# Fused transformer and RWKV-7 step on one core: the first preparation's products two gate tiles later, the wait for the gate stores moved past a barrier

## The chip, the cores and the metric

One core of one Trainium2 chip runs the whole step as one program. The metric is the device time of one execution in microseconds (us), lower is better, as the median of several runs.

## The reference

One trunk layer of a hybrid network over 512 latent and 128 context tokens with width 1024. What matters here is its first half:

```
h = modulate(rmsnorm(x))
proj = h @ w_in                      # q, k, v | u (RWKV inputs) | ga, gr (gates)
attn_o = block_attention(q, k, v)
rwkv_o = rwkv7_bidirectional(u)      # decays, rates, normed keys, then a scan per direction
merged = sigmoid(ga) * (attn_o @ w_attn_br) + sigmoid(gr) * (rwkv_o @ w_rwkv_br)
x = x + gate1 * (merged @ w_out)     # then a gated MLP in the same manner
```

## The kernel before

Activations lie feature-major: 128 features on the partitions, 644 token columns. A dense product is made in tiles of 128 output features. Each fp32 operand is split into a high and a low part, and one tile is 8 input blocks x 3 part products x 2 column halves = 48 matmuls (line 669). Two tiles make a block, whose 1 MB of weights SyncE loads into one of two buffers, ScalarE (ACT) copies to the high part (`next_hi`, L1155) and VectorE (DVE) turns into the low part (`next_lo`, L1471).

The program is written by hand, engine by engine; each engine runs its own list in order and waits on semaphores. `phase_over` (L449 to L452) is a barrier of TensorE (PE), ACT, DVE and GpSimd (POOL): each drains, adds one, and waits for all four. Barrier 1 stands ahead of the dense products of `w_in`. These are 6 tiles of q, k, v, 14 tiles of u, and, last, 16 tiles of gates in 8 blocks, numbered t = 0 to 15 here. Barrier 2 follows them, then comes the first half of the RWKV recurrence (`chunks(0)`), then barrier 3 and the attention.

Between the gate tiles the kernel prepares the recurrence of the first half (*the first preparation*, `it` = 0). PE makes ten small products of 640 columns (`prepare_product`, L933 and L934). Products 0 and 1 are sums of squared keys, one for each of two head groups, and read what ACT squares in `key_squares` once the keys have been reloaded from DRAM (`uc<-u_scratch`). Products 2 to 9 are four pairs, each pair a decay and a rate for one head group and one direction. The work of ACT and DVE on them is placed by the same tile number t:

- ACT, after it has evacuated tile 0: `key_squares`. After tile 1: `key_norm_log` (L1249) and `key_norm` (L1254) for both groups, from products 0 and 1. After tiles 2, 4, 6, 8: the tanh of both products of a pair (`prep_tanh`, L1263) and `key_factor` (L1270). After tiles 3, 5, 7, 9: `prep_decays`, three exponentials (L1277 to L1279).
- DVE at even t: `next_lo` of the next block, and at t = 2 to 9 parts of `prepare(0)` (L1595 to L1633).

PSUM holds two tiles. PE may begin tile t only when ACT has evacuated tile t-2 (L678: `pe.wait_ge(tile_evac, 2 * b + j + 1)`; ACT counts up in L1292). The list of ACT, which the change leaves as it is, is (L1283 to L1307, `g_st` being the stores of the gates):

```python
        for b in range(NBLK_U + NBLK_Q, BLK_BR):
            if b + 1 < BLK_BR:
                next_hi(b + 1, (b + 1) % 2)
            for j in range(2):
...
                ac.wait_ge(tile_done, 2 * b + j + 1)
                if f >= 1:
                    ac.wait_ge(g_st[j], 16 * f)
                ac.activation(gout[j][:, :], tile(2 * j), ACT.Tanh, scale=0.5).then_inc(tile_evac, 1)
...
                elif t < 10 and t % 2 == 0:
                    for n in range(2):
                        prep_tanh(0, t // 2 - 1, n)
                    key_factor(0, t // 2 - 1)
```

`prep_tanh` and `key_norm_log` begin with a wait for their product (`pe_prep`). Behind each evacuation POOL issues the store of the gate tile to DRAM (L614), 16 in all; their buffers `gout` are not written again before barrier 3.

Of the kernel before, what the change touches and what calls it, by code (L numbers as in the profile page):

```python
# [42 lines left out]
NBLK_U, NBLK_Q, NBLK_G = 7, 3, 8  # L43
# [110 lines left out]
def build(nc, io):  # L154
# [25 lines left out]
    def sem(name):  # L180
        return ctx.enter_context(nc.semaphore(name))
# [228 lines left out]
    g_st = [sem(f"gates_stored{s}") for s in range(2)]  # L410
# [38 lines left out]
    def phase_over(eng, n):  # L449

        eng.drain().then_inc(barrier, 1)
        eng.wait_ge(barrier, 4 * n)  # L452
# [20 lines left out]
    def paired(names):  # L473

        return [(g, name, s) for g, name in in_order(names) for s in range(2)]
# [5 lines left out]
    def at_stage(names, it, g, name):  # L481
        count = COUNT[id(names)]
        return it * len(count) + count[g, name]
# [97 lines left out]
    @block.gpsimd  # L581
    def _(gp):
        phase_over(gp, 1)
        for kv in range(2):
            gp.dma_start(k2[:, kv, 512:768], ck_d[kv]).then_inc(cache_ld, 16)
        gp.dma_start(vo[:, 4:6, :, 64:128], cv_d.rearrange("p t (g n) -> p t g n", g=2)).then_inc(cache_ld, 16)
        for a in (0, 128):
            gp.memset(vo[:, :, :, a:a + 64].rearrange("p t g n -> p (t g) n"), 1.0).then_inc(ones_set, 1)
        for i in range(6):
            for s in range(2):  # L590
                gp.wait_ge(conv_done, 2 * i + s + 1)
                gp.dma_start(u_s[2 * i + s], uout[s][:, :]).then_inc(u_st[s], 16)
        gp.wait_ge(qst_done, 5)
        gp.dma_start(qa_s[:, 0:QK], qa_made[:, 0:QK]).then_inc(qa_st[0], 16)
        gp.dma_start(nk_d, qkv[:, 4, C0:C0 + CTX]).then_inc(kv_st, 16)
        gp.dma_start(nv_d, qkv[:, 5, C0:C0 + CTX]).then_inc(kv_st, 16)
        gp.dma_start(qc_s, qkv[:, 0:4, C0:C0 + CTX]).then_inc(qa_st[1], 16)
        gp.wait_ge(vt_copied, 1)
        gp.wait_ge(cache_ld, 48)
        gp.wait_ge(ones_set, 2)  # L600
        gp.dma_start(qa_s[:, QK:QA], qa_made[:, QK:QA]).then_inc(qa_st[1], 16)
        gp.wait_ge(kv_st, 32)
        gp.wait_ge(qa_st[0], 16)
        for s in range(2):
            gp.wait_ge(u_st[s], 16 * 6)
        gp.wait_ge(qa_st[1], 32)
        u_of = u_s.rearrange("(j h) p n -> h p j n", j=3)
        for s in range(2):
            gp.dma_start(hpw[s][:, :], hpw_d[s]).then_inc(rw_ld[0][s], 16)
            gp.dma_start(uc[s][:, :, :], u_of[s]).then_inc(rw_ld[0][s], 16)  # L610
        for i in range(NBLK_G):
            for s in range(2):
                gp.wait_ge(tile_evac, 2 * i + s + 2 * (NBLK_U + NBLK_Q) + 3)
                gp.dma_start(gate_s[i, :, s, :], gout[s][:, :]).then_inc(g_st[s], 16)  # L614
        for s in range(2):
            gp.wait_ge(g_st[s], 16 * NBLK_G)
        phase_over(gp, 2)

        def presets(it):
            for g, name, s in paired(PO_ST):  # L620
                if g >= 2:
                    gp.wait_ge(pe_g[s], at_stage(PE_ST, it, g - 2, "U1"))
                gp.tensor_copy(rm[s][g % 2][:, :, :, :].rearrange("p d q n -> p (d q) n"),
                               i64.unsqueeze(1).broadcast_to([P, 4, CH])).then_inc(po_g[s], 1)

        presets(0)
        phase_over(gp, 3)
        gp.wait_ge(o_copied, 10)
        gp.dma_start(br_s[0:4].rearrange("k p n -> p k n"), aT[:, :, :]).then_inc(a_st, 16)
        gp.wait_ge(a_st, 16)  # L630
        phase_over(gp, 4)
        presets(1)
        phase_over(gp, 5)
        for k in range(8):
            if k in (4, 5):
                gp.wait_ge(rw_st[k - 4], 32)
            gp.dma_start(bld[k][:, :], br_s[k]).then_inc(b_ld[k], 16)
        for f in range(KD):
            if f >= 2:
                gp.wait_ge(mf_done, f - 1)  # L640
            gp.dma_start(gld[f % 2][:, :, :], gate_s[f]).then_inc(gl_ld[f % 2], 16)
        gp.wait_ge(tile_done, 2 * BLK_OUT)
        gp.wait_ge(mf_done, KD)
        gp.wait_ge(m_lo, KD)
        gp.dma_start(x1[:, :, :], x_d).then_inc(x1_ld, 16)
        phase_over(gp, 6)
# [3 lines left out]
    def _(pe):  # L650
# [267 lines left out]
        def prepare_product(it, n):  # L918

            tb = tbs[it]  # L920
            pe.wait_ge(prep_read, 10 * it + n + 1 + it)
            if n < 2:
                pe.wait_ge(ac_prep, 8 * it + n + 1)
                w, x = blk1, tb[8 * n][:, :]
            else:
                s = (n - 2) // 4
                pe.wait_ge(rw_ld[it][s], 32)
                pe.wait_ge(low_done, 1)
                d, low = (n - 2) % 4 // 2, n % 2
                rows = slice(64 * low, 64 * low + 64)  # L930
                w, x = wcur[s][rows, d, :], wdad[rows, :]
            at = 3072 if it else 2048 + 1024 * (n % 2)
            pe.matmul(psf[:, at:at + 512], w, x[:, 0:512], start=True, stop=True)  # L933
            pe.matmul(psf[:, at + 512:at + T], w, x[:, 512:T], start=True, stop=True).then_inc(pe_prep, 1)  # L934

        def between_gates(t):

            if t == 1:
                for s in range(2):
                    prepare_product(0, s)  # L940
            elif t % 2 == 0 and 2 <= t < 10:
                for j in range(2):
                    prepare_product(0, t + j)

        for b in range(NBLK_Q + NBLK_U, BLK_BR):
            dense_block(b, b % 2, hhi, hlo, lambda j: between_gates(2 * (b - NBLK_Q - NBLK_U) + j))
# [1040 lines left out]
```

## Time and profile before

| What | Value |
|---|---|
| median of 3 runs | 1492.28 us (1489.19 to 1492.94) |
| profiled execution: its own time, its span | 1493.71 us, 1491.9 us |
| TensorE granted clock, mean | 0.946 of full |
| busy: PE, DVE, ACT, POOL | 1336.6, 748.4, 530.3, 41.8 us |
| gate tiles, from the end of u's tiles to barrier 2 | about 208.9 to 346.2 us of the span |

The profile is one execution. Times in it count from the first instruction. The profiled execution's own time lies 1.8 us above its span (work around the instructions), and 1.4 us above the median of the runs. "PE L669 x48" is one tile.

### The profile page before, as it was taken

To read this page: it belongs to the slowest core of one execution; us is meant where nothing else is said; L and a number is where in the kernel's file an instruction comes from. 1 tells how busy PE (TensorE), PEld (TensorE's weight loads), DVE (VectorE), ACT (ScalarE), POOL (GpSimd) and SP (SyncE) were. 2 spreads that over 40 slices of the span, in tenths; PEclk is the share of its full clock that TensorE was granted. 3 is DMA by queue.
4 is the path that set the end of the run, shared out by engine and by line. 5 is a ranking of instruction groups with operands and counts; after the bars stand their busy time and mean duration, and the time that the engine had idled before them with its cause. 6 is when DMAs were issued, how large, how long until landed. Compare 5 with 4: busy or idle time off the path is not lost.

```text
span 1491.9 us, 31857 instructions
## 1 busy us (share of the span) xinstructions
PE 1336.6 (90%) x13967; PEld 1231.7 (83%) x13967; DVE 748.4 (50%) x1114; ACT 530.3 (36%) x794; POOL 41.8 (3%) x84
## 2 busy tenths in 40 slices
PE   5799998997998799879985989799999999799993
PEld 2799997997997455479965968599999999799992
DVE  3517644623554489954554622465545455344445
ACT  3535535411334343223243211363333334233332
POOL 0000010000000000000001000000000000000000
PEclk8799999998999799989996999999999999899996
DMA  9222373313000200020006477012122121022221
GB/s 397 66 94 92 105 277 128 104 54 157 8 4 3 85 0 1 1 94 8 4 11 246 145 284 294 25 61 85 60 81 84 56 84 42 14 70 78 70 64 71
DMA packets 24761, 134.58 MB, mean 90 GB/s; under 512 B 2992, under 2 KB 3632, under 8 KB 16208
## 3 DMA queue, kind: packets, MB, share of 16 engines
q1 hardware_dynamic: 19088, 103.59, 19.5%
q0 software_dynamic: 5568, 29.40, 5.2%
q8 instruction: 89, 1.46, 0.4%
q14 instruction: 16, 0.13, 0.0%
HBM read 112.66 MB, written 20.32 MB: 89 GB/s over the span
## 4 chain that ended last, share of the span: by engine, by line
PE 80%; DVE 8%; DMA 5%; ACT 3%; issue 2%; PEld 1%; POOL 0%; POOLq 0%; PEldq 0%; DVEq 0%; SPq 0%; ACTq 0%
PE ps L669 43%; PE ps L1106 10%; PE ps L822 3%; PE ps L810 3%; PE ps L790 2%; PE ps L1009 2%; PE ps L704 1%; PE ps L968 1%; PE ps L802 1%; DMA xT<-in_x 1%; DVE rden L1761 1%; PE ps L986 1%; PE ps L694 1%; PE ps L933 1%; DMA bld<-branch_scratch 1%
## 5 line engine op out<-in xcount | busy, mean ns | idle before, releaser
L669 PE MATMUL ps<-h2lo,whi 128*128 128x322 f32 x672 | 154.5, 311 | 0.7 <-ACT facc L1193 0.7
L669 PE MATMUL ps<-h2hi,wlo 128*128 128x322 f32 x672 | 155.0, 312 | 0.0
L669 PE MATMUL ps<-h2hi,whi 128*128 128x322 f32 x672 | 154.0, 310 | 0.0
L1471 DVE TENSOR_TENSOR wlo<-raw,whi 128x2048 fp32r<-128x2048 f32 x48 | 109.7, 2287 | 72.0 <-ACT whi L1155 71.8
L669 PE MATMUL ps<-hlo,whi 128*128 128x322 f32 x544 | 128.2, 317 | 1.0 <-ACT qkv L1219 1.0
L669 PE MATMUL ps<-hhi,wlo 128*128 128x322 f32 x544 | 125.8, 312 | 0.0
L669 PE MATMUL ps<-hhi,whi 128*128 128x322 f32 x544 | 125.0, 311 | 0.0
L669 PEld LDWEIGHTS ps<-h2hi,whi 128*128 128x128 f32 x672 | 114.2, 190 | 0.0
L669 PEld LDWEIGHTS ps<-h2lo,whi 128*128 128x128 f32 x672 | 113.0, 189 | 0.9 <-DVE wlo L1471 0.9
L669 PEld LDWEIGHTS ps<-h2hi,wlo 128*128 128x128 f32 x672 | 113.6, 189 | 0.0
L1515 DVE SCALAR_TENSOR_TENSOR facc<-fraw,par,facc 128x642 f32<-128x642 f32 x44 | 39.0, 887 | 140.1 <-ACT facc L1193 140.1
L1155 ACT ACTIVATE whi<-raw 128x2048 fp32r<-128x2048 f32 x48 | 91.8, 1914 | 26.4 <-PE ps L669 15.8
L1192 ACT ACTIVATE fraw<-ps 128x644 f32<-128x644 f32 x44 | 31.2, 710 | 183.8 <-PE ps L669 182.5
L669 PEld LDWEIGHTS ps<-hlo,whi 128*128 128x128 f32 x544 | 91.9, 190 | 4.1 <-issue 2.4
L669 PEld LDWEIGHTS ps<-hhi,whi 128*128 128x128 f32 x544 | 92.7, 190 | 0.0
L669 PEld LDWEIGHTS ps<-hhi,wlo 128*128 128x128 f32 x544 | 92.2, 190 | 0.0
L1106 PE MATMUL ps<-dlo,whi 128*128 128x322 f32 x352 | 81.6, 314 | 10.1 <-DVE dlo L1885 8.9
L1106 PE MATMUL ps<-dhi,wlo 128*128 128x322 f32 x352 | 82.2, 315 | 0.0
L1106 PE MATMUL ps<-dhi,whi 128*128 128x322 f32 x352 | 81.3, 312 | 0.0
L1884 DVE TENSOR_TENSOR wlo<-raw,whi 128x512 fp32r<-128x512 f32 x44 | 30.4, 692 | 92.3 <-ACT dhi L1431 92.3
L1661 DVE COPY_PREDICATED tm<-con,ps 128x256 f32<-128x256 int32 x80 | 35.5, 444 | 68.7 <-PE ps L822 67.8
L1106 PEld LDWEIGHTS ps<-dlo,whi 128*128 128x128 f32 x352 | 59.8, 192 | 10.8 <-issue 10.8
(298 smaller groups left out, 2675.2 us busy)
## 6 DMA issues: line engine op xcount, KB each, us to landing
raw<-in_wblk SPq DMA_DIRECT2D x48, 1024.0 KB, 4.8
adl<-in_wada SPq DMA_DIRECT2D x8, 2048.0 KB, 8.7
raw<-in_wdn SPq DMA_DIRECT2D x44, 256.0 KB, 2.6
adaw<-in_wada SPq DMA_DIRECT2D x4, 2048.0 KB, 17.7
gate_scratch<-gout POOLq DMA_DIRECT2D x16, 322.0 KB, 2.8
gld<-gate_scratch POOLq DMA_DIRECT2D x8, 644.0 KB, 4.2
attention_inputs_used<-attention_scratch SPq DMA_DIRECT2D x1, 5056.0 KB, 14.6
u_scratch<-uout POOLq DMA_DIRECT2D x12, 320.0 KB, 2.4
```

The lines of the kernel that those rows point to most:

```text
L669: mm = pe.matmul(o, w, v, start=first, stop=last and w is hi and x is xh[n])
L790: mm = pe.matmul(bank(b, P, P * (2 * d + q))[r], src[r, d, tokens(d, q)], ar[s][r, d, chunk_of(g, d, q), :, :].rearrange("p a n -> p (a n) ...
L810: mm = pe.matmul(bank(b1, CH, CH * (2 * d + q))[r], abm[s][g % 2][r, d, q, 0, :], tm[s][r, d, q, :], start=True, stop=True)
L822: mm = pe.matmul(bank(b0, CH, CH * (2 * d + q))[r], left, right, start=True, stop=True)
L1009: mm = pe.matmul(bank(4 + h % 2), vo_u[:, c, h // 4, at:at + P], pt[h % 2][:, c, :], start=c == 0, stop=c == 5)
L1106: mm = pe.matmul(o, w, v, start=(k == 0 and q == 0), stop=(k == FF - 1 and q == 2))
L1155: ac.activation(whi[s][:, :], raw[s][:, :], ACT.Copy).then_inc(hi_done, 1)
L1192: ac.activation(fr[j][:, :], tile(2 * j), ACT.Copy)
L1471: TT(wlo[s][:, :], raw[s][:, :], whi[s][:, :].bitcast(F32), ALU.subtract).then_inc(lo_done, 1)
L1515: st.last(STT(fa[j][:, 1:TP - 1], fr[j][:, 0:TP - 2], taps(0), fa[j][:, 1:TP - 1], ALU.mult, ALU.add))
L1661: ins = dv.copy_predicated(t1[:, :, :, :], lev[:, l - 1].unsqueeze(2).broadcast_to(each), steps_of(bank(b0, 4 * CH)))
L1884: TT(wlo[s][:, 0:512], raw[s][:, 0:512], whi[s][:, 0:512].bitcast(F32), ALU.subtract)
```

## The change

On PE, each use of `prepare_product` between the gate tiles moves two tiles down: products 0 and 1 from behind tile 1 to behind tile 3, the pairs from behind tiles 2, 4, 6, 8 to behind tiles 4, 6, 8, 10. The lists of ACT and DVE stay. On POOL, the wait for the stores of the gates moves from ahead of barrier 2 to behind the presets of `chunks(0)` (copies of an identity matrix, L623), ahead of barrier 3.

```diff
@@ gpsimd
                 gp.dma_start(gate_s[i, :, s, :], gout[s][:, :]).then_inc(g_st[s], 16)
-        for s in range(2):
-            gp.wait_ge(g_st[s], 16 * NBLK_G)
         phase_over(gp, 2)
...
         presets(0)
+        for s in range(2):
+            gp.wait_ge(g_st[s], 16 * NBLK_G)
         phase_over(gp, 3)
@@ tensor
         def between_gates(t):
 
-            if t == 1:
+            if t == 3:
                 for s in range(2):
                     prepare_product(0, s)
-            elif t % 2 == 0 and 2 <= t < 10:
+            elif t % 2 == 0 and 4 <= t < 12:
                 for j in range(2):
-                    prepare_product(0, t + j)
+                    prepare_product(0, t - 2 + j)
```

## Rows read from the trace of the kernel before

**Rows 1.** The page's part 4, the chain that ended last, by engine:

```profile
PE 80%; DVE 8%; DMA 5%; ACT 3%; issue 2%; PEld 1%; POOL 0%; POOLq 0%; PEldq 0%; DVEq 0%; SPq 0%; ACTq 0%
```

**Rows 2.** The chain in order of time, gate tiles: start, us, what:

```profile
229.05 0.84 ACT tb L1241
...
232.49 7.93 PE ps L669 x48
240.43 1.07 PE ps L933 x4
...
256.20 1.06 PE ps L933 x4
...
289.03 50.23 PE ps L669 x336
...
339.29 0.72 ACT gout L1292
...
340.29 2.46 DMA gate_scratch<-gout
...
342.84 3.34 POOLq L451
```

**Rows 3.** Timeline of TensorE: start, us, engine, line, what, [idle before <-releaser]:

```profile
226.33 1.12 PE L933 MATMUL ps<-tb,con 128*128 128x512 f32 x2 [3.16 <-ACT tb L1241]
...
230.02 2.04 PE L933 MATMUL ps<-tb,con 128*128 128x512 f32 x2 [2.14 <-ACT tb L1241]
...
232.83 0.74 PE L669 MATMUL ps<-hhi,wlo 128*128 128x322 f32 x2
233.37 0.74 PE L669 MATMUL ps<-hhi,whi 128*128 128x322 f32 x2
```

**Rows 4.** Timeline of ACT, gate tiles:

```profile
229.79 0.69 ACT L1292 ACTIVATE gout<-ps 128x644 f32<-128x644 f32 x1
230.49 1.28 ACT L1249 ACT_TABLE_LOAD   x1
231.78 1.45 ACT L1249 ACTIVATE tb<-ps 128x640 f32<-128x640 f32 x2
...
241.74 0.80 ACT L1263 ACTIVATE tb<-ps,hw 128x640 f32<-128x640 f32 x1 [0.57 <-PE ps L934]
...
243.31 0.93 ACT L1270 ACTIVATE tb<-tb,kfc 128x640 f32<-128x640 f32 x1
...
250.33 0.74 ACT L1278 ACTIVATE tb<-tb 128x650 f32<-128x650 f32 x1
```

**Rows 5.** Timeline of DVE, gate tiles:

```profile
237.75 2.29 DVE L1471 TENSOR_TENSOR wlo<-raw,whi 128x2048 fp32r<-128x2048 f32 x1 [19.21 <-ACT whi L1155]
...
245.07 0.82 DVE L1610 TENSOR_TENSOR tb<-tb 128x640 f32<-128x640 f32 x1
...
246.54 0.82 DVE L1619 SCALAR_TENSOR_TENSOR tb<-tb,tb 128x640 f32<-128x640 f32 x1
251.18 0.83 DVE L1628 SCALAR_TENSOR_TENSOR ar<-tb,tb 128x640 f32<-128x640 f32 x1 [3.82 <-ACT tb L1278]
...
254.13 2.28 DVE L1471 TENSOR_TENSOR wlo<-raw,whi 128x2048 fp32r<-128x2048 f32 x1
```

**Rows 6.** Timeline of TensorE, two products of 640 columns at full clock:

```profile
472.52 1.13 PE L908 MATMUL ps<-ysum,con 128*128 128x512 f32 x2
...
473.71 1.02 PE L908 MATMUL ps<-ysum,con 128*128 128x512 f32 x2
```

**Rows 7.** Windows: stretch, us, busy PE, PEld, DVE, ACT, POOL, granted clock, DMA:

```profile
226.00:230.00 4.00, 1.55 (x4) 0.81 (x5) 0.00 (x0) 1.14 (x3) 0.00 (x0) 0.66 0.63 245
...
350.00:352.00 2.00, 2.00 (x45) 2.00 (x44) 0.54 (x1) 0.70 (x1) 0.00 (x0) 0.96 0.84 364
```

**Rows 8.** POOL's last drain (ns) and the load issued just ahead of it (us to landing):

```profile
L451 POOLq DRAIN  x1: 11848/11848/11848, 868.5 to 868.5; - x1
...
x<-in_x POOLq DMA_DIRECT2D x1, 2576.0 KB, 11.1
```

## The prediction, made before the changed kernel ran

> **What bounds the kernel now.** I read the chain that ended last first: TensorE (PE) carries 80% of it [rows 1], so a change counts by what it does to PE's list. Next the same chain through the gate tiles [rows 2]. PE runs tile after tile there, and only two places interrupt it. The first lies behind tile 1, where the products wait for the reloaded keys: PE is idle for 3.16 us, makes product 0, idles 2.14 us more, makes product 1 [rows 3], and begins tile 2 at 232.49 [rows 2]. Tile 1 ended at 226.33 - 3.16 = 223.17, so 9.3 us lie between two tiles. The second is barrier 2: last evacuation at 339.29, store issued at 340.29, landed after 2.46 us, then 3.34 us of POOL's drain [rows 2], and PE goes on at 346.2. Both are what the change touches. Then I read the timelines of ACT and DVE [rows 4, 5], because the change moves only PE's side of a schedule that three engines share.
>
> **The first stall.** Without the products behind tile 1, PE begins tile 2 at 223.2. A tile at full clock takes 50.23/7 = 7.18 us [rows 2], so it ends at 230.4. Tile 3 needs the evacuation of tile 1, which ACT makes only after `key_squares`, from 229.79 to 230.48 [rows 4], for it waits for the same reload and squared the second group's keys from 229.05 [rows 2]. That still covers: tile 3 runs from 230.5 to 237.7. So far PE is a whole tile and more ahead.
>
> Here the gain is lost. ACT's list has the logarithms of products 0 and 1 right behind that evacuation, ahead of the next high part and of the evacuation of tile 2. The products now come behind tile 3. At 1.19 us each (473.71 - 472.52) [rows 6] they end at 240.2. The table for the logarithm loads ahead of the wait: it began at 230.49, before product 1 was done at 232.49 [rows 2, 4]. What follows product 1 is one logarithm, both exponentials, the high part and the low part of block 2's weights. Before, that took from 232.49, in the middle of the two logarithms (231.78, 1.45 us [rows 4]), to 237.75 + 2.29 = 240.04, so 7.55 us [rows 2, 5], hidden under tile 2. Now tile 4 needs these weights, and nothing is left for PE to do. It stands still for 7.6 us and begins tile 4 at 247.8.
>
> The granted clock then is low. After the idle time behind tile 1 it fell: 0.66 on average from 226 to 230 [rows 7], and tile 2 took 7.93 us instead of 7.18 [rows 2]. After barrier 2 it was back at full only about 350.1 (0.96 over 350 to 352) [rows 7], 3.9 us after PE resumed. At low clock a pair of matmuls takes 233.37 - 232.83 = 0.54 us [rows 3] against 7.18/24 = 0.30, so 44% of such time is lost: 3.9 us cost 1.7. I take 1.8 for tile 4, with the 0.75 of tile 2 as lower end. Tile 4 ends at 247.8 + 7.18 + 1.8 = 256.8. Before, it ended at 256.20 [rows 2]. So the removed stall of 9.3 us comes back as another one, and PE is 0.6 us late, with one pair of products more before it.
>
> **The four pairs.** Let a pair of products begin at time 0, behind tile t (4, 6, 8, 10). From 240.43 [rows 2] the first tanh began 1.31 us later (241.74), and `key_factor` ended at 243.31 + 0.93, so 3.81 us later [rows 4]. Before, ACT did this after it had evacuated t, one tile ahead of need, and only then the evacuation t+1, which only tile t+3 needed. Now ACT's wait for the pair stands two tiles earlier in its list than the products in PE's. Behind it is the evacuation of tile t-1 (0.69 us [rows 4]), and PE needs it for tile t+1 at once. So tile t+1 begins at 3.81 + 0.69 = 4.50 us, instead of 1.4 us (what two tiles leave of 256.20 - 240.43 = 15.77 [rows 2]). That is a stall of 3.1 us in each of four pairs.
>
> DVE is late too. The low part of the weights for tile t+2 stands behind its preparation parts. L1619 ended 6.93 us after the pair began (246.54 + 0.82 - 240.43), with L1610 done at 5.46. ACT's two exponentials, 0.74 us each [rows 4], follow L1610 and are done by about the same time. From the start of L1628 to the end of `wlo` is 254.13 + 2.28 - 251.18 = 5.23 us [rows 5]. So the weights are ready at 12.2 us for the first direction, and one operation of 0.74 us later, at 12.9, for the second (L1622 is added). Tile t+1 ends at 4.50 + 7.18 = 11.7 at full clock. PE would wait 0.5 or 1.2 us more, 3.4 us over four pairs. But 3.16 us of idling brought the clock down before [rows 3, 7], so tile t+1 will run partly at low clock. That covers the wait for DVE, and what counts is the larger of the two. I take 1.4 us per pair, between 0.75 (tile 2) and 1.75 (after barrier 2): 5.6 us in all, and 3.4 to 7.0 as bounds.
>
> Sum from 256.8: 4 x 4.50 + 11 tiles x 7.18 + 5.6 = 102.6, so tile 15 ends at 359.4 instead of 289.03 + 50.23 = 339.26 [rows 2]: **+20.1 us**. From tile 11 on no product is waited for, and ACT catches up.
>
> **The barrier.** POOL no longer waits 2.46 us for the last store, but it must still issue it (0.5 us) and drain. So 2.0 us go if the drain of 3.34 us [rows 2] only begins earlier. What that drain does isn't shown. The one drain right behind an issued load took 11.85 us with the load landing after 11.1, so it ended 0.8 us behind the landing [rows 8]. By that pattern it would end at 340.29 + 2.46 + 0.8 = 343.5 and save 2.6. It saves nothing if the 3.34 us always follow the landing, and 5.3 (2.46 + 3.34 - 0.5) if they vanish. I take **-2.0 us**. The wait in its new place is free: the stores landed 2.5 us after their issue, and POOL's next need is barrier 3, behind the whole recurrence half. The Trainium skill (DMA: Bandwidth & Descriptors, Anatomy of one DMA) gives such a store a fixed 2.0 us plus 0.75 for its size, an estimate of 2.8 that would make this term -2.3. The row decides.
>
> Everything behind barrier 2 only shifts. Sum: +20.1 - 2.0 = +18.1. Against the profiled execution's own 1493.71 that is 1511.8; against the median of 1492.28 it is **1510.4 us**, slower by 1.2%.
>
> **Rivals.**
> 1. *Faster: ACT's waits don't reach PE.* Tiles 2 to 15 would run from 223.17 with only the products between: 223.17 + 14 x 7.18 + 2.4 + 4 x 1.4 = 331.7, which is 7.6 us earlier, and 2.0 at the barrier: 1482.7. For it speaks the visible stall of 9.3 us, which does go. It needs the evacuation of tile t-1 done before the pair behind tile t is waited for. Against it: in ACT's list the evacuation of tile 3 stands behind the pair's tanh (241.74 [rows 4]), and PE's wait at L678 allows two tiles. The Trainium skill (TensorE: Matmul & The Clock Gate, Architectural detail) calls ACT's queue strict FIFO; this trace shows nothing of ACT out of order. Chance 0.05.
> 2. *No change: only the first wait is felt.* PE is 0.6 late at tile 4, adds 1.4 for the extra pair, and wins 2.0 at the barrier: 1492.3. This needs ACT to regain its lead after tile 4, which it could only if it were not itself waiting for products that PE makes later. Chance 0.06.
> 3. *Slower still: the clock stays down.* Behind tile 1 it was low from about 227.3 (0.66 over 226 to 230) to past 233.4 [rows 3, 7], over 6 us. If each pair's stall costs 6.8 us at low clock, 3.0 us instead of 1.4, it becomes 4 x 1.6 = 6.4 more: 1516.8. Against it: that gap held two idle times, a pair has one. Chance 0.08.
>
> My forecast has 0.81.
>
> **Range and chances.** 0.3% (4.5 us) is about what a measurement of this kernel can tell from no change. The forecast's own bounds: barrier saves 5.3 (-3.3), clock 3.4 instead of 5.6 (-2.2), tile 4 loses 0.75 (-1.05): 1503.9. Upwards: nothing at the barrier (+2.0), 7.0 (+1.4): 1513.8. Rival 3 and the spread of the runs take it to 1516. Range 1503 to 1516. Faster 0.05, within 0.3% 0.06, slower 0.89.
>
> **What would show it.** Right: PE runs tiles 1, 2, 3 without a gap and then idles some 7.6 us for `wlo`; `key_norm_log` begins about 8 us later, near 239; four gaps of about 3.1 us behind the products, released by ACT's `gout`; the low part of the next weights arriving as PE ends the tile after; tile 15 ending near 359; POOL's drain starting about 0.5 us after the last issue. Wrong: no gap behind the pairs, or ACT evacuating t-1 ahead of the products' wait. If the gaps are there and the total is off, then the clock after them or the drain was mis-sized.

## The result and the profile after

The changed kernel takes 1511.62 us (median of 4 runs, 1510.58 to 1512.59) against 1491.2 us for the kernel before (4 runs). The ratio is 1.0132, 95% interval 1.012 to 1.0144: slower by 20.4 us. The profiled execution took 1511.57 us, its span is 1509.8 us.

The chain of waits through the gate tiles, to hold against [rows 2]:

```profile
230.55 7.41 PE ps L669 x48
...
243.54 1.81 ACT whi L1155
245.35 0.02 issue
245.37 2.30 DVE wlo L1471
247.67 0.04 issue
247.71 9.36 PE ps L669 x48
257.07 1.06 PE ps L933 x4
...
260.78 0.69 ACT gout L1292
261.48 0.04 issue
261.52 16.08 PE ps L669 x96
...
282.39 16.09 PE ps L669 x96
...
302.99 16.10 PE ps L669 x96
...
323.59 30.39 PE ps L669 x192
...
362.13 4.18 POOLq L451
```

Tile 3 starts at 230.55, with tile 2 ended just before. Then the chain leaves PE for ACT's and DVE's split of the weights (243.54, 245.37), and tile 4 starts at 247.71. Where [rows 2] had a pair of products every 15.8 us with tiles right behind it, ACT's `gout` now stands between a pair and the next tile. Two tiles behind it take 16.1 us instead of 14.4.

Who waited for whom in this stretch (us in total, times, longest):

```profile
PE ps L669 <- ACT gout L1292: 13.1, 4, 3.5
...
PE ps L669 <- DVE wlo L1471: 7.6, 1, 7.6
PE ps L884 <- POOLq L451: 5.2, 1, 5.2
```

Four waits behind the pairs make 13.1 us, the one behind tile 3 makes 7.6, and barrier 2 costs 5.2 instead of the 6.96 from tile 15 to 346.22. ACT's timeline shows the other side:

```profile
229.81 0.69 ACT L1292 ACTIVATE gout<-ps 128x644 f32<-128x644 f32 x1
230.52 1.28 ACT L1249 ACT_TABLE_LOAD   x1
239.08 0.70 ACT L1249 ACTIVATE tb<-ps 128x640 f32<-128x640 f32 x1 [7.28 <-PE ps L934]
...
245.24 0.69 ACT L1292 ACTIVATE gout<-ps 128x644 f32<-128x644 f32 x1
258.38 0.79 ACT L1263 ACTIVATE tb<-ps,hw 128x640 f32<-128x640 f32 x1 [12.45 <-PE ps L934]
...
260.78 0.69 ACT L1292 ACTIVATE gout<-ps 128x644 f32<-128x644 f32 x1
...
361.15 0.71 ACT L1292 ACTIVATE gout<-ps 128x644 f32<-128x644 f32 x1 [6.44 <-PE ps L669]
```

ACT waits 12.45 us for a pair, then does the preparation first and the evacuation of tile 3 last, at 260.78. PE starts tile 5 right behind it. Tile 15 is done at 361.1, which is 21.9 us later than before. The granted clock (seventh figure of a row, the one behind POOL's):

```profile
248.00:252.00 4.00, 4.00 (x16) 4.00 (x17) 0.53 (x1) 0.00 (x0) 0.00 (x0) 0.50 0.80 274
252.00:256.00 4.00, 4.00 (x28) 4.00 (x27) 0.00 (x0) 0.00 (x0) 0.00 (x0) 0.99 0.02 4
256.00:262.00 6.00, 2.84 (x19) 2.00 (x18) 2.69 (x7) 2.99 (x4) 0.24 (x1) 1.00 0.00 0
262.00:270.00 8.00, 8.00 (x46) 8.00 (x44) 7.24 (x8) 3.89 (x5) 0.84 (x2) 0.79 0.21 83
```

It is 0.50 (1.2 of 2.4 GHz) for the first 4 us of tile 4, behind 7.6 us in which TensorE stood still, and 0.79 on average over 8 us behind the first pair's gap.

### The profile page after: what moved, and what is told of

Its sections match the earlier page's. It is cut to its first block, busy times and chain, and to the rows that moved or that the text cites. A ratio compares the mean times of both kernels' runs of the same rounds, so it can differ in the third digit from the quotient of the medians.

```text
span 1509.8 us, 31857 instructions
## 1 busy us (share of the span) xinstructions
PE 1343.2 (89%) x13967; PEld 1237.5 (82%) x13967; DVE 748.7 (50%) x1114; ACT 529.6 (35%) x794; POOL 41.9 (3%) x84
## 4 chain that ended last, share of the span: by engine, by line
PE 79%; DVE 8%; DMA 4%; ACT 4%; issue 2%; PEld 1%; POOL 0%; POOLq 0%; PEldq 0%; SPq 0%; ACTq 0%; DVEq 0%
PE ps L669 42%; PE ps L1106 10%; PE ps L822 3%; PE ps L810 3%; PE ps L790 2%; PE ps L1009 2%; PE ps L704 1%; PE ps L968 1%; PE ps L802 1%; DMA xT<-in_x 1%; DVE rden L1761 1%; PE ps L694 1%; PE ps L986 1%; PE ps L658 1%; PEld ps L694 1%
## 5 line engine op out<-in xcount | busy, mean ns | idle before, releaser
L669 PE MATMUL ps<-hlo,whi 128*128 128x322 f32 x544 | 131.2, 323 | 21.8 <-ACT gout L1292 13.1
L1155 ACT ACTIVATE whi<-raw 128x2048 fp32r<-128x2048 f32 x48 | 91.7, 1913 | 25.6 <-PE ps L669 15.8
L1106 PE MATMUL ps<-dlo,whi 128*128 128x322 f32 x352 | 81.5, 314 | 10.1 <-DVE dlo L1885 8.9
L1661 DVE COPY_PREDICATED tm<-con,ps 128x256 f32<-128x256 int32 x80 | 35.6, 445 | 67.3 <-PE ps L822 66.4
```

The source lines that it names most:

```text
L669: mm = pe.matmul(o, w, v, start=first, stop=last and w is hi and x is xh[n])
L1106: mm = pe.matmul(o, w, v, start=(k == 0 and q == 0), stop=(k == FF - 1 and q == 2))
L1155: ac.activation(whi[s][:, :], raw[s][:, :], ACT.Copy).then_inc(hi_done, 1)
L1661: ins = dv.copy_predicated(t1[:, :, :, :], lev[:, l - 1].unsqueeze(2).broadcast_to(each), steps_of(bank(b0, 4 * CH)))
```

## The experiments

All compare with the kernel before, run with them on the same chip. The first four ran together (before: 1492.93 us), the other four together (before: 1492.25 us). The changed kernel was in neither group; its loss of 20.4 us is against its own runs of before. Intervals are 95%. Each experiment has one profile.

**products_only**: the change on PE alone, without the one on POOL.

```diff
-            if t == 1:
+            if t == 3:
...
-            elif t % 2 == 0 and 2 <= t < 10:
+            elif t % 2 == 0 and 4 <= t < 12:
                 for j in range(2):
-                    prepare_product(0, t + j)
+                    prepare_product(0, t - 2 + j)
```

> Only the products move two tiles later; the wait for the stores stays ahead of barrier 2. Theory (ACT's waits cost PE the stalls; the profile of the changed kernel has tile 15 end 21.9 us later): slower than before by 21 to 23 us, so 1.5 to 2 us slower than the changed kernel. Rival (the two parts act on each other): anything outside 20 to 24 us.

Measured 1513.33 us, ratio 1.0132 (1.0113 to 1.015): 20.4 us slower. The whole loss comes with the products. The size is just under the band of 21 to 23. The median lies 1.7 us above the changed kernel's, but so does that of before in this group (1492.93 against 1491.2 us). Against its own before each kernel loses 20.4 us, so these runs don't show the 1.5 to 2 us that were expected between the two. In the profile TensorE waits 7.0 us for POOL at barrier 2 here and 5.2 us in the changed kernel.

**wait_only**: the change on POOL alone.

```diff
-        for s in range(2):
-            gp.wait_ge(g_st[s], 16 * NBLK_G)
         phase_over(gp, 2)
...
         presets(0)
+        for s in range(2):
+            gp.wait_ge(g_st[s], 16 * NBLK_G)
```

> Only the wait for the stores of the gates moves behind the presets. Theory: faster by 1.7 to 2.0 us, 0.12%, since POOL's drain begins 2.4 us earlier and lasts somewhat longer; too small for more than a hint in the timed runs, but in the profile TensorE goes on 5.2 us after tile 15 instead of 6.9. Rival (the drain has to wait until the store has landed and then lasts its 3.3 us): 6.9 us again, no change.

Measured 1489.33 us (12 runs), ratio 0.9974 (0.9964 to 0.9984). In its chain POOL drains and PE goes on behind:

```profile
336.94 4.18 POOLq L451
...
341.16 4.53 PE ps L884 x80
```

Tile 15's evacuation began at 336.0 here, so PE goes on 5.2 us later, as forecast. The time, however, fell by 3.6 us (2.4 to 5.4), more than the 1.7 us that this place shows. The profiles differ in more places. The first tile of `w_in` began at 67.17 us here and at 69.72 before, and tile 2 at 228.98 instead of 232.49, both ahead of all that was changed. Such an early start shows also in `pairs_only`, `filled` and `one_tile_last_stores` (67.3 to 67.6, against 68.8 to 69.8 in the others). The recurrence half up to the attention was 1.2 us shorter (142.3 against 143.5 us), but so it was in `one_tile` (142.1), which has the old wait. Whether an early start belongs to a kernel or to one execution isn't known, so the timed surplus over 1.7 us stays open.

**pairs_only**: products 0 and 1 stay behind tile 1, only the pairs go two tiles later.

```diff
             if t == 1:
...
-            elif t % 2 == 0 and 2 <= t < 10:
+            elif t % 2 == 0 and 4 <= t < 12:
                 for j in range(2):
-                    prepare_product(0, t + j)
+                    prepare_product(0, t - 2 + j)
```

> Products 0 and 1 stay behind tile 1, the four pairs go two tiles later, the old wait for the stores. Theory: the old gap behind tile 1 stays, tile 4 waits for nothing, and each pair costs 3.1 us of waiting and 1.7 us of low clock: 4 x 4.8 = 19 us slower than before (18 to 20.5). Rival (the loss comes from products 0 and 1 only): no change against before.

Measured 1512.39 us, ratio 1.0135 (1.0115 to 1.0154): 19.5 us slower. Its waits:

```profile
PE ps L669 <- ACT gout L1292: 13.1, 4, 3.5
PE ps L884 <- POOLq L451: 7.0, 1, 7.0
PE ps L933 <- ACT tb L1241: 4.1, 2, 2.8
```

The same 13.1 us in four waits, and no wait for `wlo`. The four pairs make nearly all of the loss: 19.5 us here, and 20.4 us with products 0 and 1 moved too, a difference that lies within the intervals. Products 0 and 1 only exchange one gap for another.

**one_tile**: the products one tile later, behind tiles 2, 3, 5, 7 and 9; the old wait on POOL.

```diff
-            if t == 1:
+            if t == 2:
...
-            elif t % 2 == 0 and 2 <= t < 10:
+            elif t % 2 == 1 and 3 <= t < 11:
                 for j in range(2):
-                    prepare_product(0, t + j)
+                    prepare_product(0, t - 1 + j)
```

> Products one gate tile later (behind tiles 2, 3, 5, 7, 9) with the old wait for the stores. Theory (PE may run two tiles ahead of ACT's evacuations, so a shift of one tile is free and a shift of two is not): no gap behind the pairs, the old gap of 9.3 us behind tile 1 gone too, tile 15 ends near 331.7 instead of 339.3: 7 to 8 us faster than before. Rival (any product later than ACT's wait for it costs, in proportion to the shift): about half of the loss of two tiles, 10 us slower.

Measured 1483.93 us, ratio 0.9932 (0.9917 to 0.9947): 9.0 us faster (7 to 8 expected, interval 7.9 to 12.4). The chain:

```profile
214.94 15.18 PE ps L669 x102
230.12 0.86 PE ps L933 x2
...
232.28 7.14 PE ps L669 x48
...
288.02 43.09 PE ps L669 x288
331.13 0.72 ACT gout L1292
```

PE runs without a gap from the u tiles to the last gate tile, which ends at 331.1 (331.7 expected). The rival, a loss in proportion to the shift, is out. One tile is free and gains the gap of 9.3 us; two lose 20.

**three_lists**: two tiles later, but ACT's and DVE's parts of the preparation go with the products.

```diff
-            if t == 1:
+            if t == 3:
...
-            elif t % 2 == 0 and 2 <= t < 10:
+            elif t % 2 == 0 and 4 <= t < 12:
...
-                elif t == 1:
+                elif t == 3:
                     for s in range(2):
                         key_norm_log(0, s)
...
-                elif t < 10 and t % 2 == 0:
+                elif 4 <= t < 12 and t % 2 == 0:
                     for n in range(2):
-                        prep_tanh(0, t // 2 - 1, n)
+                        prep_tanh(0, t // 2 - 2, n)
...
-            if 2 <= t < 10:
-                for part in range((4 if t % 4 == 2 else 3) if t % 2 == 0 else 2):
+            if 4 <= t < 12:
+                for part in range((4 if t % 4 == 0 else 3) if t % 2 == 0 else 2):
```

> Products two tiles later, and with them ACT's logarithms, tanh, key factors and exponentials and DVE's parts of prepare(0), all two tiles later; the old wait for the stores. Theory (the loss comes from the distance between the lists and not from the later place of the products): no gap behind the products, none behind tile 1, tile 15 ends near 331.7: 7 to 9 us faster than before, as with one tile. Rival (late products are themselves too late for the recurrence): the gap moves to barrier 2 and the time stays that of before or more.

Measured 1485.29 us, ratio 0.9953 (0.9938 to 0.9968): 7.0 us faster, at the edge of the expected 7 to 9. The waits of PE for ACT shrink to one:

```profile
PE ps L669 <- ACT gout L1292: 0.4, 1, 0.4
```

Tile 15's evacuation begins at 331.07 (331.7 expected), and barrier 2 costs the 7.0 us of before. So two tiles later is not in itself too late for the work behind. What costs is the distance between PE's list and ACT's.

**filled**: the changed kernel with matmuls of constants in PE's gaps. They write columns of the bank of tile t that the tile leaves free; the tile's signal comes behind them. Their results are never read.

```diff
+        def keep_busy(t, n):
+            for _ in range(n):
+                mm = pe.matmul(bank(2 * (t % 2), FLAT), blk1, con[:, 0:FLAT], start=True, stop=True)
+            mm.then_inc(tile_done, 1)
...
             if t == 3:
                 for s in range(2):
                     prepare_product(0, s)
+                keep_busy(t, 22)
...
                     prepare_product(0, t - 2 + j)
+                keep_busy(t, 9)
```

> The changed kernel with extra matmuls of constants (190 columns) in TensorE's gaps, 22 behind products 0 and 1, 9 behind each pair, so that TensorE is busy while it waits; their results are never read. Theory (each gap costs its length and 1.7 us of low clock behind it, and under that low clock lies DVE's late low part of the weights): granted clock 1.0 from tile 3 on, the 6.8 us of low clock behind the pairs and 1.8 to 2.2 behind tile 3 go, and 3.4 us of waiting for the low part appear: 5 to 6 us faster than the changed kernel, so 15 us slower than before. Rival (the clock has no part in it): no faster than the changed kernel, rather 1 us slower. Rival (nothing hides under the low clock): 9 us faster than the changed kernel.

Measured 1507.65 us, ratio 1.0102 (1.0086 to 1.0117): 15.4 us slower than before, so 5.0 us less loss than the changed kernel (20.4, from another group of runs). Clock and waits:

```profile
248.00:252.00 4.00, 4.00 (x29) 4.00 (x28) 0.00 (x0) 0.00 (x0) 0.00 (x0) 1.00 0.55 229
...
262.00:270.00 8.00, 7.58 (x52) 7.32 (x51) 3.96 (x4) 1.12 (x2) 0.54 (x1) 1.00 0.48 160
```

```profile
PE ps L669 <- DVE wlo L1480: 3.1, 5, 1.0
PE ps L669 <- ACT gout L1301: 1.4, 2, 1.0
```

The clock stays at 1.00, and the tiles behind the gaps are done sooner. Now PE waits five times for the low part (`wlo`, L1480 here), 3.1 us in all. The first, 0.5 us, is the end of the gap behind tile 3. The other four, 2.6 us (3.4 expected), stand a tile behind each pair, where the changed kernel's waits show none: it hid them under its low clock. The two groups of runs alone would leave room for 0.4 to 8.7 us. The profiles narrow it: ACT's last evacuation begins at 355.3 instead of 361.1, and of these 5.8 us 1.4 come from an earlier tile 3 (229.16 instead of 230.55), so 4.4 are the filling's. Neither rival fits, 0 or less or 9. Not all of it reaches the end of the profile, whose span is only 3.3 us shorter than the changed kernel's (1506.5 against 1509.8): the recurrence half took 144.1 us here and 142.3 there, which the filling doesn't explain.

**last_stores**: the kernel before, but the stores of the last block are issued behind barrier 2.

```diff
-        for i in range(NBLK_G):
+        for i in range(NBLK_G - 1):
...
-        for s in range(2):
-            gp.wait_ge(g_st[s], 16 * NBLK_G)
         phase_over(gp, 2)
...
         presets(0)
+        for s in range(2):
+            gp.dma_start(gate_s[NBLK_G - 1, :, s, :], gout[s][:, :]).then_inc(g_st[s], 16)
+        for s in range(2):
+            gp.wait_ge(g_st[s], 16 * NBLK_G)
         phase_over(gp, 3)
```

> The kernel before, but the two stores of the last gate block are issued behind the presets, and awaited there with the others. Theory (barrier 2 is held by POOL alone: evacuation, issue, landing or drain): POOL reaches its drain early, and TensorE goes on some 1.1 us after tile 15 instead of 6.9: 5 to 6 us faster than before. Rival (POOL's drain of 3.3 us is a cost of the barrier and not of the store just issued): 3 us at most.

Measured 1484.79 us, ratio 0.9945 (0.9932 to 0.9959): 7.5 us faster (6.1 to 10.1), more than the expected 5 to 6. The chain at the barrier, and POOL's drain (ns):

```profile
339.17 0.71 ACT gout L1294
339.88 0.04 ACTq L451
...
339.97 2.55 PE ps L886 x80
```

```profile
L451 POOLq DRAIN  x1: 5237/5237/5237, 325.9 to 325.9; - x1
```

PE goes on 0.8 us after tile 15, released by ACT. POOL's drain, behind the store of tile 13, takes 5.2 us but is over at 331.2. So of the 6.96 us between tile 15 and 346.22 nearly all was POOL's, and the change removed 1.7.

The other gain lies right behind the barrier, in the clock. Before, the 80 matmuls behind the barrier (L884, L886 here) took 4.31 us, behind a wait of 6.96 us. Here they take 2.55, behind a wait of 0.8 us. These are the kernel before and, last, this run:

```profile
346.22 4.31 PE L884 MATMUL ps<-con,uc 64*64 64x64 f32 x80 [6.96 <-POOLq L451]
346.00:348.00 2.00, 1.78 (x34) 1.78 (x36) 0.70 (x2) 0.00 (x0) 1.55 (x4) 0.50 1.08 324
...
339.90:341.90 2.00, 1.93 (x66) 1.94 (x68) 0.69 (x2) 0.45 (x1) 1.61 (x4) 1.00 1.09 324
```

The granted clock is 1.00 where it was 0.50. The 6.1 us of an earlier start and these 1.8 us make 7.9, and 7.5 were measured.

**one_tile_last_stores**: `one_tile` and `last_stores` together.

```diff
-        for i in range(NBLK_G):
+        for i in range(NBLK_G - 1):
...
-            if t == 1:
+            if t == 2:
...
-            elif t % 2 == 0 and 2 <= t < 10:
+            elif t % 2 == 1 and 3 <= t < 11:
...
+            gp.dma_start(gate_s[NBLK_G - 1, :, s, :], gout[s][:, :]).then_inc(g_st[s], 16)
```

> Products one tile later and the last two stores issued behind the presets. Both gains add: 7.6 from the first gap and 5.8 from the barrier, 12 to 15 us faster than before. If one eats the other, 9 or less.

Measured 1475.28 us, ratio 0.9889 (0.9874 to 0.9905): 17.0 us faster than before (14.2 to 18.8), above the expected 12 to 15, though the interval reaches into it. The gains add: measured alone they were 9.0 and 7.5 us, so 16.5. This is the fastest version, 2.4% under the changed kernel.

## Why the prediction was right

The forecast was 1510.4 us, 18.1 us over the median then known. The difference turned out as 20.4 us, and the median of before, with one more run, as 1491.2. So the loss was 2.3 us larger than forecast, and the baseline 1.1 us lower. That the time came out only 1.2 us off is in part luck. In the profiles tile 15 is 21.9 us late (20.1 forecast) and TensorE leaves barrier 2 20.1 us late (18.1 forecast). Behind it the changed kernel's profile regains 2.2 us, 1.1 of them in the recurrence half, so the spans differ by only 17.9 us. The forecast had "everything behind barrier 2 only shifts"; what regains them isn't shown, and the profiled execution of before was itself 2.5 us over its median.

- *The gap behind tile 1 goes, tile 3 starts at 230.5, and a gap of 7.6 us opens for `wlo`*: tile 3 started at 230.55, the wait was 7.6 us. `pairs_only` shows what this exchange is worth. The pairs alone cost 19.5 us, and with products 0 and 1 moved as well it is 20.4 (`products_only`), so the removed gap of 9.3 us brought nothing that can be measured.
- *Low clock on tile 4*: 1.8 us forecast; the tile took 9.36 instead of 7.18, 2.2 us.
- *Each tile behind a pair begins 4.50 us after the pair*: 261.52 - 257.07 = 4.45, then 4.79, 4.51 and 4.51, and the four waits are 13.1 us where 4 x 3.1 = 12.4 were forecast. `one_tile` and `three_lists` show that the cause is the one named: with the products no more than one tile behind ACT's wait, or ACT's wait moved along, these waits are gone.
- *The larger of low clock and late weights, 5.6 us for four pairs*: this was the most mis-sized term. Two tiles took 16.08 to 16.10 instead of 14.36, and the last stretch, 323.59 to 361.1 for five tiles, 1.6 more than 35.9: 6.8 us, near the stated upper bound of 7.0. That both causes lie on each other is shown by `filled`. Without the low clock, 2.6 us of waiting for `wlo` come out behind the pairs.
- *Barrier: -2.0*: 5.2 instead of 7.0 us, so -1.7 in the profile. From the issue of the last store to the end of the drain it was 340.29 to 346.18, 5.9 us, and is 362.15 to 366.31, 4.2 us: the drain begins earlier but lasts longer (4.17 against 3.33 us). Why `wait_only` gained 3.6 us in the timed runs is open.
- *Rivals*: the faster one (ACT's waits don't reach PE) would need PE able to run more than two tiles ahead. That ACT's waits don't reach PE holds for a shift of one tile, as `one_tile` shows. "Only the first wait is felt" is refuted by `pairs_only`. The slower one, a clock that stays down for 6.8 us, didn't come: 0.79 over 262 to 270 is 3.4 us at half clock. Its own 1516.8 us lay above the stated range, which ended at 1516. The Trainium skill (TensorE: Matmul & The Clock Gate, Architectural detail) calls ACT strict FIFO, and ACT's evacuation of tile 3 at 260.78, behind the preparation though tile 3 was done at 237.96, agrees.

## What to carry to other kernels

When a producer's step is moved later in one engine's list, look at what the consumer's list has behind the wait for it. If that includes freeing a buffer that the producer needs, each step of the shift uses up one buffer. Here, with two tiles in PSUM, one tile was free and two tiles cost 4.9 us per pair (19.5 us for four in `pairs_only`). That such a shift is free up to the depth of the buffering less one is argued from the lists; no other depth was tried. Move the lists together, or by less than the depth. At a barrier ask what the last engine still has to do before it signals: here issuing the last two stores behind it gained 7.5 us, in part because TensorE, idle for only 0.8 us, kept its clock.

## What the runs showed of the hardware that was not expected

At barrier 2 POOL's drain took several microseconds in every kernel: 3.33 us when the last store had been awaited first, 4.17 us directly behind the issue of the last store, 5.24 and 4.77 us behind the store of tile 13 in the two kernels with late last stores. At barrier 4, behind a single awaited store, it took 0.14 us. What it does in that time was not tried.

Behind each of the four stalls of 3.2 to 3.5 us between pair and tile the clock was low: 0.57 to 0.60 on average over the first 4 us, 0.97 to 1.00 over the next 4. Behind the 7.0 us at barrier 2 before the change the granted clock was 0.50. Behind the 0.8 us that `last_stores` left there it was 1.00. Matmuls of constants whose results are not used kept the clock at 1.00 through the gaps behind the products. Against the changed kernel that bought back 5.0 of 20.4 us.
